# A hybrid decoder step on one core: eight raw weight slots instead of four, and merge heads written out on two engines

## What is computed

```python
h = _rms_norm(x, norm_g)
z = h @ w_in                        # 2048 x 15368
# z is split into the inputs of four branches, their gates and merge_logits
y_ret  = head_rms(retention(rope(q), rope(k), v)) * silu(ret_gate)
y_gdn  = rms_norm(gated_delta(l2norm(q), l2norm(k), v, g, beta)) * silu(gdn_gate)
y_sc   = sc_b * causal_conv(sc_c * sc_h) * silu(sc_gate)
y_pool = mix(causal_means(pool_u) - pool_u) * pool_scale * silu(pool_gate)
proj   = einsum('btnc,ncd->btnd', [y_ret, y_gdn, y_sc, y_pool], w_branch)
merged = sum(sigmoid(merge_logits) * proj, axis=branch)
out    = x + merged @ w_out
```

## Time and profile before

| | before |
|---|---|
| runs, us | 2023.88, 2019.29, 2022.82 |
| median, us | 2022.82 |
| profiled execution, us | 2024.55 |
| its span from first to last instruction, us | 2022.5 |
| mean granted clock of TensorE | 0.994 |

### The profile page before, as it was taken

How to read it: one execution, slowest core, us unless ns; L and a number is a source line. 1 busy time by engine, 2 the same in 40 slices (tenths; PEclk the granted TensorE clock), 3 DMA queues, 4 the chain that set the end, 5 groups by cost and what they waited for, 6 DMA issues and landing times.

```text
span 2022.5 us, 49537 instructions
## 1 busy us (share of the span) xinstructions
PE 1981.2 (98%) x16190; PEld 1962.1 (97%) x16190; DVE 1343.4 (66%) x2610; ACT 1112.0 (55%) x2046; POOL 180.5 (9%) x342
## 2 busy tenths in 40 slices
PE   9999999999999999999999999999999999999996
PEld 8999999999999999999999999999999999999996
DVE  7887566666566566666688766676555555566666
ACT  6556556546464555555555655665464546455554
POOL 1111110100001010000011111001000001000000
PEclk9999999999999999999999999999999999999998
DMA  7555565555555546665556555555545555566554
GB/s 239 186 167 173 165 188 167 185 159 158 165 160 163 162 148 177 180 180 181 182 182 187 171 163 178 175 171 177 171 152 168 150 161 158 157 174 181 178 180 163
DMA packets 183818, 348.03 MB, mean 172 GB/s; under 512 B 20656, under 2 KB 21040, under 8 KB 183696
## 3 DMA queue, kind: packets, MB, share of 16 engines
q1 hardware_dynamic: 178128, 326.45, 53.0%
q0 software_dynamic: 5568, 19.80, 3.1%
HBM read 333.61 MB, written 12.56 MB: 171 GB/s over the span
## 4 chain that ended last, share of the span: by engine, by line
PE 89%; DVE 4%; ACT 3%; issue 2%; DMA 2%; SPq 0%; DVEq 0%; ACTq 0%; POOL 0%; POOLq 0%
PE acc L1427 27%; PE acc L1428 26%; PE acc L1429 26%; DMA raw<-w_stream 2%; DVE wlo L878 1%; PE side L1653 1%; PE side L1627 1%; ACT whi L557 1%; PE side L1651 1%; PE side L1634 1%; PE side L1541 1%; PE side L1497 1%; DVE wide L901 1%; PE side L1488 0%; PE side L1644 0%
## 5 line engine op out<-in xcount | busy, mean ns | idle before, releaser
L878 DVE TENSOR_TENSOR wlo<-raw,whi 128x512 fp32r<-128x512 f32 x1219 | 828.2, 695 | 475.6 <-ACT whi L557 467.8
L557 ACT ACTIVATE whi<-raw 128x512 fp32r<-128x512 f32 x1219 | 750.5, 627 | 634.5 <-PE acc L1429 537.7
L1427 PE MATMUL acc<-act_hi,whi 128*128 128x264 f32 x3328 | 970.1, 291 | 21.6 <-issue 16.1
L1429 PE MATMUL acc<-act_hi,wlo 128*128 128x264 f32 x3328 | 945.5, 284 | 0.0
L1428 PE MATMUL acc<-act_lo,whi 128*128 128x264 f32 x3328 | 945.1, 284 | 0.0
L1427 PEld LDWEIGHTS acc<-act_hi,whi 128*128 128x128 f32 x3328 | 629.8, 189 | 30.1 <-issue 19.7
L1428 PEld LDWEIGHTS acc<-act_lo,whi 128*128 128x128 f32 x3328 | 630.5, 189 | 0.9
L1429 PEld LDWEIGHTS acc<-act_hi,wlo 128*128 128x128 f32 x3328 | 627.2, 188 | 0.0
L1427 PE MATMUL acc<-y_hi,whi 128*128 128x264 f32 x1536 | 440.1, 287 | 0.3 <-DVE wlo L878 0.3
L1428 PE MATMUL acc<-y_lo,whi 128*128 128x264 f32 x1536 | 435.4, 283 | 0.0
L1429 PE MATMUL acc<-y_hi,wlo 128*128 128x264 f32 x1536 | 434.9, 283 | 0.0
(11 more groups left out here) (270 smaller groups left out, 1413.2 us busy)
## 6 DMA issues: line engine op xcount, KB each, us to landing
raw<-w_stream SPq DMA_DIRECT2D x1220, 256.0 KB, 2.8
state<-ret_in POOLq DMA_DIRECT2D x8, 512.0 KB, 5.4
s_ret<-state POOLq DMA_DIRECT2D x8, 512.0 KB, 4.6
state<-gdn_in POOLq DMA_DIRECT2D x8, 512.0 KB, 5.9
s_gdn<-state POOLq DMA_DIRECT2D x8, 512.0 KB, 4.6
x<-x_in SPq DMA_DIRECT2D x4, 528.0 KB, 6.7
y_out<-wide SPq DMA_DIRECT2D x4, 396.0 KB, 2.4
hist_out<-hist POOLq DMA_DIRECT2D x2, 468.0 KB, 3.0
```

The lines of the kernel that those rows point to most:

```text
L557: sc.activation(whi[:, s, :], raw[:, s, :], ACT.Copy).then_inc(hi_ready, 1)
L878: ve.tensor_tensor(wlo[:, s, :], raw[:, s, :], whi[:, s, :].bitcast(F32), ALU.subtract).then_inc(lo_ready, 1)
L1427: mm(acc[bank][:, 0:N], w_h, hi[:, k0 + k, :], start=first and k == 0, stop=False)
L1429: op = mm(acc[bank][:, 0:N], w_l, hi[:, k0 + k, :], start=False, stop=last and k == UK - 1)
```

## The change

`raw` gets eight slots (`RAW`), while `whi` and `wlo` keep four (`RING`). SP asks for units 0 to 7 in the opening, two behind each quarter of `x`; after that come the first constants and the second part of the parameters, then eight reloads with the other constants behind every second one, and then a loop of eight reloads a turn.

```diff
+RAW = 8
...
+def slot_phase(start, i, per):
+
+    if isinstance(i, int):
+        return (start + i * per) % RAW, (start + i * per) // RAW
+    assert per % RAW == 0 and start % RAW == 0
+    return 0, start // RAW + i * (per // RAW)
...
-        raw = sb("raw", [RING, UC])
+        raw = sb("raw", [RAW, UC])
...
-        raw_loaded = [sem(f"raw_loaded{i}") for i in range(RING)]
+        raw_loaded = [sem(f"raw_loaded{i}") for i in range(RAW)]
...
-                if q < 2:
-                    for s in range(2 * q, 2 * q + 2):
-                        sp.dma_start(raw[:, s, :], w_stream[s]).then_inc(raw_loaded[s], 16)
+                for s in range(2 * q, 2 * q + 2):
+                    sp.dma_start(raw[:, s, :], w_stream[s]).then_inc(raw_loaded[s], 16)
...
                 sp.wait_ge(lo_ready, u + s + 1 + RING)
-                sp.dma_start(raw[:, s, :], w_stream[u + RING + s]).then_inc(raw_loaded[s], 16)
+                sp.dma_start(raw[:, s, :], w_stream[u + RAW + s]).then_inc(raw_loaded[s], 16)
...
-            for s in range(RING):
-                reload(s, 0)
             constants(0)
             sp.dma_start(par[:, Q_WAB:Q_END], params[:, Q_WAB:Q_END]).then_inc(par_loaded, 16)
-            for s in range(RING):
-                reload(s, RING)
-                constants(s + 1)
-            with sp.Fori(0, DEPTH * UNITS // RING - 2) as r:
-                u = sp.snap((r + 2) * RING)
-                for s in range(RING):
+            for s in range(RAW):
+                reload(s, 0)
+                if s % 2:
+                    constants(s // 2 + 1)
+            with sp.Fori(0, DEPTH * UNITS // RAW - 1) as r:
+                u = sp.snap((r + 1) * RAW)
+                for s in range(RAW):
                     reload(s, u)
...
                 def split(a, b):
                     for j in range(a, b):
-                        s = j % RING
-                        act.wait_ge(raw_loaded[s], rb + 16 * (j // RING + 1))
+                        r = (lead + j) % RAW
+                        act.wait_ge(raw_loaded[r], rb + 16 * ((lead + j) // RAW + 1))
                         act.wait_ge(unit_used, ub + j + 1)
-                        sc.activation(whi[:, s, :], raw[:, s, :], ACT.Copy).then_inc(hi_ready, 1)
+                        sc.activation(whi[:, j % RING, :], raw[:, r, :], ACT.Copy).then_inc(hi_ready, 1)
...
-                with act.Fori(0, BT) as h:
+                for h in range(BT):
                     it = held(act, l * BT + h)
                     ub, split = splitter(l, OFF_M, h, MTURN)
...
-                with act.Fori(0, BT - 1) as h:
+                for h in range(BT - 1):
                     gdn_merge_turn(h, False)
...
-                with dve.Fori(0, BT) as h:
+                for h in range(BT):
                     it = held(dve, l * BT + h)
                     ub, split = splitter(l, OFF_M, h, MTURN)
...
-                with dve.Fori(0, BT - 1) as h:
+                for h in range(BT - 1):
                     gdn_merge_turn(h, False)
...
-    w_stream = np.concatenate([w_stream[opening], w_stream[2 * UB:], w_stream[:RING]])
+    w_stream = np.concatenate([w_stream[opening], w_stream[2 * UB:], w_stream[:RAW]])
...
-    nc = bacc.Bacc("TRN2", target_bir_lowering=False, num_devices=1)
+    nc = bacc.Bacc("TRN2", target_bir_lowering=False, num_devices=1, dynamic_dma_scratch_size=4096)
```

More of the change, by code:

```diff
@@ L377, in constants @@
                 sp.dma_start(con[:, a:b], consts[:, a:b]).then_inc(con_loaded, 16)
-            for s in range(RING):
-                reload(s, 0)
             constants(0)
             sp.dma_start(par[:, Q_WAB:Q_END], params[:, Q_WAB:Q_END]).then_inc(par_loaded, 16)
-            for s in range(RING):
-                reload(s, RING)
-                constants(s + 1)
-            with sp.Fori(0, DEPTH * UNITS // RING - 2) as r:
-                u = sp.snap((r + 2) * RING)
-                for s in range(RING):
+            for s in range(RAW):
[5 more added lines that the diff above has]
+                for s in range(RAW):
                     reload(s, u)
-            for s in range(RING):
-                sp.wait_ge(raw_loaded[s], (DEPTH * UNITS // RING + 1) * 16)
+            for s in range(RAW):
+                sp.wait_ge(raw_loaded[s], (DEPTH * UNITS // RAW + 1) * 16)
             pieces_out = ((0, 3, final_ready), (FINAL_DVE, 13, final_pool), (3, 6, final_ready), (6, 9, final_ready),
@@ L549, in splitter @@
                 ub = held(act, l * UNITS + off + i * per)
-                rb = held(act, (l * (UNITS // RING) + off // RING + i * (per // RING)) * 16)
+                lead, turns = slot_phase(l * UNITS + off, i, per)
+                rb = held(act, turns * 16)
                 def split(a, b):
                     for j in range(a, b):
-                        s = j % RING
-                        act.wait_ge(raw_loaded[s], rb + 16 * (j // RING + 1))
+                        r = (lead + j) % RAW
+                        act.wait_ge(raw_loaded[r], rb + 16 * ((lead + j) // RAW + 1))
                         act.wait_ge(unit_used, ub + j + 1)
-                        sc.activation(whi[:, s, :], raw[:, s, :], ACT.Copy).then_inc(hi_ready, 1)
+                        sc.activation(whi[:, j % RING, :], raw[:, r, :], ACT.Copy).then_inc(hi_ready, 1)
                 return ub, split
@@ L872, in splitter @@
                 ub = held(dve, l * UNITS + off + i * per)
+                lead = slot_phase(l * UNITS + off, i, per)[0]
                 def split(a, b):
                     for j in range(a, b):
-                        s = j % RING
+                        s, r = j % RING, (lead + j) % RAW
                         dve.wait_ge(hi_ready, ub + j + 1)
-                        ve.tensor_tensor(wlo[:, s, :], raw[:, s, :], whi[:, s, :].bitcast(F32), ALU.subtract).then_inc(lo_ready, 1)
+                        ve.tensor_tensor(wlo[:, s, :], raw[:, r, :], whi[:, s, :].bitcast(F32), ALU.subtract).then_inc(lo_ready, 1)
                 return ub, split
```

## The result

| | before | after |
|---|---|---|
| median, us | 2022.82 | 2033.42 |
| lowest to highest, us (runs) | 2019.29 to 2024.04 (5) | 2031.78 to 2036.23 (5) |
| profiled execution, us | 2024.55 | 2036.23 |
| its span, us | 2022.5 | 2033.7 |
| mean granted clock of TensorE | 0.994 | 0.993 |

The changed kernel is slower: the ratio of its time to the time before is 1.0055 [1.0041, 1.0069].

A forecast was written before the change was run, and what follows sets the result against it. PE, busy 1981.2 of 2022.5 us, was taken to set the time; 1.5 us from the opening and 0.5 from constants for registers made 2.0 us less than the median 2022.82, 2020.8 us, range 2015 to 2026.

The forecast's parts named there:

- Unrolling ACT's and DVE's merge heads: Merge heads of both layers, written out on ACT and DVE: loading the straight code costs PE 0 us.
- The cover: Merge heads: `whi` and `wlo` lead PE by up to three units, 4.3 us, which hides code loading.
- Constants for registers: Merge heads: waits with a constant instead of a register save 0.5 us, between 0 and 1.2 us.
- The opening: First 60 us: earlier requests for units 8 to 11 save PE 1.5 us, between 0 and 3.4 us.
- the steady part: Reloads with eight raw slots: ACT's load waits shrink, but PE waits for no `wlo` made late by loads; 0 us.
- PE's loop: Merge heads: PE's loop is untouched, so its six waits at ends of turns, 16.1 us, stay; change 0.
- The rival that eight slots would remove the boundary waits: Ends of merge-head turns: eight slots and unrolled code remove 16.1 us of waits plus 6 us of half clock, 2001 us; chance 0.06.
- The scratch: POOL's DMAs with smaller scratch: state loads have 8 us of cover, so cost 0 and no gain.
- The rival of slow straight code: Six further merge heads: ACT or DVE stops at each new code block, 24 us slower, 2045 us; chance 0.05.
- The clock: PE's half clock after three of six long waits loses 6 us; no difference taken, 3 us either way in the range.

The follow-up runs named there:

- the first experiment: The changed kernel with a one-column exponential added on ACT at the top of each merge head: 2020.31 us, ratio 0.9988.
- 2002.42: The kernel before with only PE's merge heads written out, ACT's and DVE's loops and four raw slots kept: 2002.42 us, ratio 0.9897.
- 1999.39: The changed kernel with PE's merge heads written out too and a one-column exponential on ACT at the top of each head: 1999.39 us, ratio 0.9892.
- the first set: The unchanged kernel before, measured beside the first four follow-up runs: 2023.36 us (2018.91 to 2028.41, 23 runs).

## Why the prediction was wrong

It gave 2020.8 us with a range of 2015 to 2026 and a chance of 0.09 for slower; the kernel came out at 2033.42. By its own steps:

- **Unrolling ACT's and DVE's merge heads: this step failed.** "Cost taken: 0" rested on code loading alone: the first head is code run for the first time, and it is as fast as the second. For code loading that holds; both engines' straight code is free (2020.31 with all of it, 2022.3 with DVE's alone). But the first head of before is a turn of the loop, its table load on the loop's first line included, and so it could not stand for a head written out. What the step left out is that an engine's code is not only what the kernel writes: ACT's table loads are placed by the block they stand in, and the edit changes the block. The load on L557 was in the trace of before to be seen, on a line that only copies. Measured: +11 us where 0 stood.
- **The cover.** The lead of `whi` and `wlo`, "up to three units ..., 4.3 us", was named as what hides a delay. At units 8 and 11 it was 0.67 and 0.1 us: ACT's splits there stand behind its wait for PE's score rows, and a delay of 1.4 us went through almost whole. A lead is not a property of a stage but of a place in it.
- **Constants for registers, 0.5 us.** Not measurable (0.9998 [0.9986, 1.0009]).
- **The opening, 1.5 us: right.** Unit 11 starts at 28.25 instead of 29.82, unit 21 at 43.32 instead of 45.42, 2.1 us earlier. ACT's waits for raw loads, 94.5 us in 107 places before, are one of 1.1 us. Over all executions profiled here, unit 21 starts at 44.39 to 47.11 with four slots and at 43.10 to 44.41 with eight. The two ranges just touch. Eight slots without any unrolling weren't tried, so the gain in time stands on these starts, on the 2020.31 of the first experiment and on the 3.0 us between 2002.42 and 1999.39, and how much of it the slots have alone is open. The 0 for the steady part agrees with PE's list as long as the boundary waits are there; without them four slots let that one of 1.1 us through.
- **PE's loop, 0: right,** with its reading of the earlier trace rows. The waits sum to 16.1 us again, queue 8 moves the 26 blocks of the earlier trace rows in the same stretch, and writing out PE's loop alone removes them. The rival that eight slots would remove the boundary waits is out; its price, 16.1 + 6 us, is nearly what the right edit brings (20.9 us).
- **The scratch, 0: right** (1.0004 [0.9992, 1.0016]).
- **The rival of slow straight code** had the sign and the engine right, and not the mechanism: queue 14 moves 43 blocks in all instead of 27, and the first experiment, with all of that straight code, loses nothing by it.
- **The clock, 3 us either way: right in kind.** The lower clock follows five boundaries after and three before, about 2 us. The remark that the clock stays up where the wait is shorter fits the six waits of before, and not the runs: in the first experiment it fell behind the wait of 1.9 us (1477.8 to 1481.2 at 0.50), and with DVE's heads written out it stayed at 1.00 behind one of 3.1 us (699.5 to 702.0). What decides it stays open.

## What to carry to other kernels

Before a loop on ACT is written out, or a function moved, list the table loads by line and ask which of them stand at the top of a loop body: written out, such a load went here to the first function that needs the table, and 1.28 us that were free can land between PE's result and the work that PE waits for. A one-column activation of the right function, put where the engine has time, fixes its place.

A unit that was ready 3 us before PE started it was not what PE waited for, whatever the view of waits names; look at the instruction queue of that engine. And a lead is to be read at the very place where the delay would fall, from the starts of the instructions there.

## What was not expected of the hardware

- The spread of the runs goes with the clock. Of the 23 runs of before in the first set, the three with a mean granted clock of 0.996 took 2018.91 to 2022.11 us, the one with 0.990 took 2028.41. Where PE's boundary waits are gone, the clock is 0.997 in each of the twelve runs (three kernels), and four runs of one kernel lie within 0.8 to 1.1 us.
- A jump back on PE costs more than its wait. In the profiled runs with such waits the lower clock follows three to five of the six boundaries (12.4 us in the earlier trace rows, 16.3 after), and writing out one loop of four turns took 20.9 us off the median (2023.36 - 2002.42).
- The same instruction of 1.28 us costs nothing at the top of a head and 1.4 us some nine us later, behind the score rows.
